# Down biases summed in the routing stage, and a last stage with three VectorE passes per tile

## What is computed

```python
h2 = rmsnorm(x, norm2_g) * (1.0 + sc2) + sh2
logits = h2 @ w_router + b_router
top_vals, top_idx = top_k(logits, 4)
weights = softmax(top_vals)
# for each token n and each of its four experts e, with weight w:
#   y[n] += w * (act(h2[n] @ w_gate_up[e] + b_gate_up[e]) @ w_down[e] + b_down[e])
x = x + gt2 * y
out = rmsnorm(x, final_norm_g)
```

## Time and profile before

| | us |
|---|---|
| median of 3 runs | 2881.35 |
| lowest and highest | 2880.42 and 2886.74 |
| profiled execution, whole time | 2879.79 |
| its span in the profile | 2877.9 |
| last stage (`phase_combine`), of the span | 2825.9 to 2877.9 |
| routing stage (`phase_route`), of the span | 1009.4 to 1037.6 |

### The profile page before, as it was taken

How to read it: one execution, slowest core, us unless ns; L and a number is a source line. 1 busy time by engine, 2 the same in 40 slices (tenths; PEclk the granted TensorE clock), 3 DMA queues, 4 the chain that set the end, 5 groups by cost and what they waited for, 6 DMA issues and landing times. The chain is left out here.

```text
span 2877.9 us, 42547 instructions
## 1 busy us (share of the span) xinstructions
PE 2649.8 (92%) x12459; PEld 2139.7 (74%) x12460; DVE 1822.0 (63%) x2667; ACT 1468.4 (51%) x2138; POOL 353.7 (12%) x428
## 2 busy tenths in 40 slices
PE   4999799996799759999999999999999999999994
PEld 4888677775677648888888888888777777887771
DVE  5332144544555576566666665666699999999995
ACT  5221144442333245555555544555587777777771
POOL 0000011101001220111111111111111111111110
PEclk7999899997799769999999999999999999999995
DMA  6652222212334276666666666666699999999975
GB/s 238 240 200 82 98 81 70 70 41 91 106 123 163 96 260 239 216 214 215 213 217 213 217 224 216 225 225 219 221 361 366 360 370 363 364 363 365 367 270 189
DMA packets 188364, 631.14 MB, mean 219 GB/s; under 512 B 24931, under 2 KB 50709, under 8 KB 170245
## 3 DMA queue, kind: packets, MB, share of 16 engines
q1 hardware_dynamic: 162240, 554.07, 52.4%
q0 software_dynamic: 24832, 71.95, 9.8%
q10 hardware_dynamic: 1220, 4.21, 0.4%
HBM read 575.44 MB, written 64.73 MB: 222 GB/s over the span
## 5 line engine op out<-in xcount | busy, mean ns | idle before, releaser
L2535 DVE TENSOR_TENSOR e_gu_lo<-gu_raw,e_gu_hi 128x1024 fp32r<-128x1024 f32 x564 | 673.5, 1219 | 176.0 <-ACT e_gu_hi L2374 148.9
L83 PE MATMUL e_pgu<-e_gu_hi,e_x_hi 128*128 128x512 f32 x1568 | 638.9, 407 | 5.6 <-DVE e_x_lo L2565 5.6
L85 PE MATMUL e_pgu<-e_gu_hi,e_x_lo 128*128 128x512 f32 x1568 | 615.6, 393 | 0.0
L84 PE MATMUL e_pgu<-e_gu_lo,e_x_hi 128*128 128x512 f32 x1568 | 613.6, 391 | 0.0
L2374 ACT ACTIVATE e_gu_hi<-gu_raw 128x1024 fp32r<-128x1024 f32 x564 | 571.7, 1055 | 29.3 <-PEq L2766 19.9
L2541 DVE TENSOR_TENSOR e_dn_lo<-dn_raw,e_dn_hi 128x1024 fp32r<-128x1024 f32 x280 | 333.0, 1218 | 16.7 <-ACT e_dn_hi L2380 16.7
L85 PEld LDWEIGHTS e_pgu<-e_gu_hi,e_x_lo 128*128 128x128 f32 x1568 | 294.9, 188 | 64.3
L83 PEld LDWEIGHTS e_pgu<-e_gu_hi,e_x_hi 128*128 128x128 f32 x1568 | 296.0, 189 | 53.2 <-issue 5.9
L84 PEld LDWEIGHTS e_pgu<-e_gu_lo,e_x_hi 128*128 128x128 f32 x1568 | 296.4, 189 | 48.2
L83 PE MATMUL e_pdn<-e_dn_hi,e_a_hi 128*128 128x512 f32 x784 | 309.1, 394 | 22.3 <-DVE e_a_lo L2569 21.6
L85 PE MATMUL e_pdn<-e_dn_hi,e_a_lo 128*128 128x512 f32 x784 | 306.4, 391 | 0.0
(11 more groups left out here) (424 smaller groups left out, 3913.9 us busy)
## 6 DMA issues: line engine op xcount, KB each, us to landing
gu_raw<-in_w_gate_up_dram SPq DMA_DIRECT2D x560, 512.0 KB, 5.6
dn_raw<-in_w_down_dram SPq DMA_DIRECT2D x140, 1024.0 KB
wada_later<-in_w_ada_dram SPq DMA_DIRECT2D x32, 512.0 KB, 4.0
gu_bias<-hidden_bias SPq DMA_DIRECT2D x42, 256.0 KB, 10.8
win_raw<-in_w_in_dram POOLq DMA_DIRECT2D x5, 2048.0 KB
proj_by_token<-out_stage SPq DMA_DIRECT2D x32, 256.0 KB, 3.1
wg_raw<-in_w_in_dram POOLq DMA_DIRECT2D x16, 512.0 KB, 4.8
gates_transposed<-g_stage POOLq DMA_DIRECT2D x32, 256.0 KB, 2.3
```

The lines of the kernel that those rows point to most:

```text
L83: pe.matmul(out, a[0], w[0], start=first, stop=False)
L84: pe.matmul(out, a[0], w[1], start=False, stop=False)
L85: return pe.matmul(out, a[1], w[0], start=False, stop=last)
L2535: dve.tensor_tensor(gu_lo[:, b, 2 * j:2 * j + 2], gu_raw[:, b, 2 * j:2 * j + 2].rearrange("p k g n -> p k (g n)"), gu_hi[:, b, 2 * j:2 * j ...
```

## The change

In `phase_out` the eight stores of zeros to the tokens' rows are gone; the one to the spare rows stays. In `phase_route` SyncE first loads `b_down` (128 KB); TensorE makes, for each of the 8 tiles, the product of turned weights and `b_down` into one PSUM tile `pb` of 1024 columns; ScalarE copies it to one of two buffers; and SyncE stores it to the tile's rows of `m.y_sum`. So the experts' scatters add to the bias sums. TensorE's first product stands before the counts' matmuls of line 1930, and the other seven behind the last weights' turn. Each product but the first waits until ScalarE has copied the one before. ScalarE's first copy stands before that of line 1922. SyncE waits for the last stores at the end of the stage.

At the end of `phase_experts` the residual of seven tiles is loaded ahead, into both halves of `gu_raw`, and `b_down` is not. In `phase_combine` TensorE has nothing to do, VectorE's add from PSUM is gone, every tile has its own `y` buffer, and all eight loads of `y` and the one of the eighth residual are issued at once.

```diff
 # phase_out, SyncE
-                sp.dma_start(m.y_sum[rows, :].rearrange("p (a n) -> p a n", a=4), zeros).then_inc(zero_out, 16)
-                if t == 0:
                     sp.dma_start(m.y_sum[SEQ:SEQ + P, :].rearrange("p (a n) -> p a n", a=4), zeros).then_inc(zero_out, 16)
...
-            sp.wait_ge(zero_out, 16 * (NT + 1))
+            sp.wait_ge(zero_out, 16)
 # phase_route
+        pb = m.psum(ctx, "pb5", [P, D])
...
         def _(sp):
+            sp.dma_start(down_bias[:], m.b_down[0]).then_inc(down_in, 16)
...
+            for t in range(NT):
+                sp.wait_ge(sum_out, t + 1)
+                sp.dma_start(m.y_sum[t * P:(t + 1) * P, :], biased[:, t % 2]).then_inc(sum_stored[t % 2], 16)
             sp.wait_ge(bias_kept, 32)
+            for b in range(2):
+                sp.wait_ge(sum_stored[b], 16 * (NT // 2))
...
         def _(act):
...
+            def keep_sums(t):
+                act.wait_ge(summed, t + 1)
+                if t >= 2:
+                    act.wait_ge(sum_stored[t % 2], 16 * (t // 2))
+                act.activation(biased[:, t % 2], pb[:], ACT.Copy).then_inc(sum_out, 1)
+            keep_sums(0)
             act.wait_ge(bias_up, 1)
             act.activation(m.bias_hl[:], braw[:], ACT.Copy).then_inc(bias_hi, 1)
+            for t in range(1, NT):
+                keep_sums(t)
...
         def _(pe):
+            def sum_biases(t):
+                if t:
+                    pe.wait_ge(sum_out, t)
+                else:
+                    pe.wait_ge(down_in, 16)
+                for half in range(2):
+                    cols = slice(half * N, (half + 1) * N)
+                    ins = pe.matmul(pb[:, cols], m.wcT[:, t], down_bias[:, cols], start=True, stop=True)
+                ins.then_inc(summed, 1)
...
             pe.matmul(pc[0:NE, 0:1], m.so_far[:, LAST], m.ones[:, 0:1], start=True, stop=True).then_inc(filled, 1)
+            sum_biases(0)
             pe.wait_ge(cum_in, 1)
...
             turn_weights(pe, m, r, LAST, 0)
+            for t in range(1, NT):
+                if t == LAST:
+                    pe.wait_ge(r.wc_kept, 1)
+                sum_biases(t)
 # phase_experts, SyncE's end
-            sp.dma_start(m.c_bd, m.b_down[0]).then_inc(once_in, 16)
             sp.dma_start(m.c_gf, m.final_g.rearrange("(a d) -> a d", a=1).to_broadcast([P, D])).then_inc(once_in, 16)
-            for t in range(2):
+            for t in range(C_AHEAD):
                 sp.dma_start(m.c_x2[:, t], m.x2[t * P:(t + 1) * P, :]).then_inc(once_in, 16)
-            wait_apart(sp, once_in, 64)
+            wait_apart(sp, once_in, 16 * C_AHEAD + 16)
 # phase_combine, with C_AHEAD = 7
         def _(sp):
             for t in range(NT):
-                b = t % 2
-                if t >= 2:
-                    sp.wait_ge(x3, t - 1)
-                sp.dma_start(y[:, b], m.y_sum[t * P:(t + 1) * P, :]).then_inc(y_in[b], 16)
-                if t >= 2:
-                    sp.dma_start(x2[:, b], m.x2[t * P:(t + 1) * P, :]).then_inc(y_in[b], 16)
...
-                    ins = pe.matmul(ps[:, t % 2, cols], m.wcT[:, t], bd[:, cols], start=True, stop=True)
-                ins.then_inc(biased, 1)
+                sp.dma_start(y[:, t], m.y_sum[t * P:(t + 1) * P, :]).then_inc(y_in[t], 16)
+            for t in range(C_AHEAD, NT):
+                sp.dma_start(late[:, t - C_AHEAD], m.x2[t * P:(t + 1) * P, :]).then_inc(x2_in, 16)
...
-                dve.tensor_tensor(acc[:, b], y[:, b], ps[:, b], ALU.add).then_inc(summed, 1)
-                dve.wait_ge(summed, t + 1)
-                dve.tensor_tensor(acc[:, b], acc[:, b], m.gate2[:], ALU.mult).then_inc(gated, 1)
+                dve.tensor_tensor(acc[:, b], y[:, t], m.gate2[:], ALU.mult).then_inc(gated, 1)
                 dve.wait_ge(gated, t + 1)
-                dve.tensor_tensor(acc[:, b], acc[:, b], x2[:, b], ALU.add).then_inc(x3, 1)
+                if t >= C_AHEAD:
+                    dve.wait_ge(x2_in, 16 * (t - C_AHEAD + 1))
+                dve.tensor_tensor(acc[:, b], acc[:, b], residual(t), ALU.add).then_inc(x3, 1)
```

More of the change, by code:

```diff
@@ L1864, in phase_route @@
         braw = sb(ctx, "r_braw", [P, FF], F32)
+        biased = sb(ctx, "r_biased", [P, 2, D], F32)
+        down_bias = sb(ctx, "r_down_bias", [NE, D], F32)
         pq = sb(ctx, "r_pq", [P, 1], F32)
@@ L1881, in phase_route @@
         bias_hi = sem("r_bias_hi")
+        down_in = sem("r_down_in")
+        summed = sem("r_summed")
+        sum_out = sem("r_sum_out")
+        sum_stored = [sem(f"r_sum_stored{i}") for i in range(2)]
         block = ctx.enter_context(nc.Block())
@@ L2640, in _ @@
             low_a(total - 1)
+C_AHEAD = 7
 def phase_combine(nc, m):
@@ L2648, in phase_combine @@
     with ExitStack() as ctx:
-        y = sb(ctx, "c_y", [P, 2, D], F32)
-        bd, gf, x2 = m.c_bd, m.c_gf, m.c_x2
+        y = sb(ctx, "c_y", [P, NT, D], F32)
+        late = sb(ctx, "c_x2", [P, NT - C_AHEAD, D], F32)
         acc = sb(ctx, "c_acc", [P, 2, D], F32)
@@ L2654, in phase_combine @@
         nrm = sb(ctx, "c_nrm", [P, NT, 4], F32)
[L2655 to L2658, removed]
+        y_in = [sem(f"c_y_in{i}") for i in range(NT)]
+        x2_in = sem("c_x2_in")
         gated = sem("c_gated")
@@ L2666, in phase_combine, with residual @@
         block = ctx.enter_context(nc.Block())
+        def residual(t):
+            return m.c_x2[:, t] if t < C_AHEAD else late[:, t - C_AHEAD]
         @block.sync
@@ L2670, in _ @@
             for t in range(NT):
-                b = t % 2
-                if t >= 2:
-                    sp.wait_ge(x3, t - 1)
-                sp.dma_start(y[:, b], m.y_sum[t * P:(t + 1) * P, :]).then_inc(y_in[b], 16)
-                if t >= 2:
-                    sp.dma_start(x2[:, b], m.x2[t * P:(t + 1) * P, :]).then_inc(y_in[b], 16)
-        @block.tensor
-        def _(pe):
-            for t in range(NT):
-                if t >= 2:
-                    pe.wait_ge(summed, t - 1)
-                for half in range(2):
-                    cols = slice(half * N, (half + 1) * N)
-                    ins = pe.matmul(ps[:, t % 2, cols], m.wcT[:, t], bd[:, cols], start=True, stop=True)
-                ins.then_inc(biased, 1)
+                sp.dma_start(y[:, t], m.y_sum[t * P:(t + 1) * P, :]).then_inc(y_in[t], 16)
+            for t in range(C_AHEAD, NT):
+                sp.dma_start(late[:, t - C_AHEAD], m.x2[t * P:(t + 1) * P, :]).then_inc(x2_in, 16)
         @block.vector
@@ L2696, in scale @@
                     dve.wait_ge(out_done[b], 16 * (t // 2))
-                dve.scalar_tensor_tensor(out=res[:, b], in0=acc[:, b], scalar=nrm[:, t, 2:3], in1=gf, op0=ALU.mult, op1=ALU.mult).then_inc(done, 1)
+                dve.scalar_tensor_tensor(out=res[:, b], in0=acc[:, b], scalar=nrm[:, t, 2:3], in1=m.c_gf, op0=ALU.mult, op1=ALU.mult).then_inc(done, 1)
             for t in range(NT):
                 b = t % 2
-                dve.wait_ge(y_in[b], 32 * (t // 2) + 16)
-                dve.wait_ge(biased, t + 1)
+                dve.wait_ge(y_in[t], 16)
                 if t >= 2:
                     dve.wait_ge(done, t - 1)
-                dve.tensor_tensor(acc[:, b], y[:, b], ps[:, b], ALU.add).then_inc(summed, 1)
-                dve.wait_ge(summed, t + 1)
-                dve.tensor_tensor(acc[:, b], acc[:, b], m.gate2[:], ALU.mult).then_inc(gated, 1)
+                dve.tensor_tensor(acc[:, b], y[:, t], m.gate2[:], ALU.mult).then_inc(gated, 1)
                 dve.wait_ge(gated, t + 1)
-                dve.tensor_tensor(acc[:, b], acc[:, b], x2[:, b], ALU.add).then_inc(x3, 1)
+                if t >= C_AHEAD:
+                    dve.wait_ge(x2_in, 16 * (t - C_AHEAD + 1))
+                dve.tensor_tensor(acc[:, b], acc[:, b], residual(t), ALU.add).then_inc(x3, 1)
                 if t:
```

4 lines of the change are left out of this document (2 added, 2 removed).

## The result

| | before | after |
|---|---|---|
| median of 4 runs each (us) | 2883.51 | 2901.77 |
| lowest, highest (us) | 2880.42, 2886.74 | 2898.07, 2903.95 |
| profiled execution (us), its span | 2879.79, 2877.9 | 2902.47, 2900.9 |

The ratio of the times is 1.0060, with a 95% interval of 1.0044 to 1.0075: slower by 12.7 to 21.6 us on 2883.5. The forecast was +16.0.

What follows compares the result with a forecast made beforehand. VectorE was taken to pace the last stage, GpSimd to end the routing stage. Terms 0, +26.2, +1.2 and -11.4 give +16.0, turning the profiled 2879.79 into 2895.8 us; 2897 was forecast for the median, range 2888 to 2904.

Steps and rivals of the forecast that it cites:

- phase_out at 0: In phase_out: dropping eight stores of zeros changes nothing, 0 us, with 0.5 us of gain as the other end.
- The routing stage, +26.2: Routing stage: seven product-and-copy rounds of 5.00 us in series, then the last store, delay the experts by 26.2 us.
- The hop from TensorE to ScalarE: Routing stage: time from TensorE's end to ScalarE's start in each round, taken as 0.15 us, between 0.05 and 0.26.
- The tail, +1.2: End of the experts' stage: longer loads share the DMA engines evenly with the last scatter, costing 1.2 us.
- third rival: Routing stage or tail: stores wait behind 6 MB of weights, or the scatter is starved for 4 us; 2900 to 2903, chance 0.12.
- The last stage, -11.4: Last stage: scalings come 4.02 us apart instead of 5.27, and the stage gains 11.4 us.
- T: Last stage: start of the first gate pass, put at 2829.05 against 2829.84, with tile 0's data there at 2829.0.
- The experts' stage, 0: Experts' stage from 1038 to 2826 us: keeps its instructions, so no change apart from its tail.
- The first (a clock that rises): Routing stage: TensorE's clock rises to 2.4 GHz, seven rounds take 22 us; +3 net, 2884.4, chance 0.08.
- The second: Routing stage: the sums are hidden under GpSimd's drain, needing rounds of 1.25 us; -10.2 us, 2871, chance 0.04.
- The fourth: Last stage: passes become bound by ScalarE; each 0.1 us beyond its cover costs 0.7 us in all; no chance given.
- cover of 0.55: Last stage: ScalarE needs 1.93 us to the next root while VectorE has passes of 2.48, leaving 0.55 us.

Runs made afterwards that it cites:

- e1: The kernel before, unedited, profiled a second time: 2879.14 us.
- e7: The changed kernel with two residual tiles loaded ahead instead of seven: 2903.99 us (one run).
- e3: The changed kernel with two PSUM buffers for the products instead of one: 2888.79 us, ratio to before 1.0031.
- e6: The changed kernel, unedited, profiled and timed again: 2898.09 us, ratio to before 1.0064.
- e10: The changed kernel with the products over 96 rows of other data instead of 32, sums wrong: 2904.30 us (one run).
- e4: The changed kernel with the products over 128 rows of other data instead of 32, sums wrong: 2889.39 us (one run).
- e8: e5 with eight buffers instead of two for the sums to be stored: 2883.15 us, ratio to before 1.0002.
- e11: The kernel before with GpSimd adding the residual, six residuals loaded ahead, products still in the last stage: 2884.03 us, ratio 1.0006.
- e2: The kernel before with only the last stage and its loads ahead changed, down biases left out: 2874.22 us, ratio 0.9973.
- e5: The changed kernel with three fp32r products packed into one for seven tiles, two made early, two PSUM buffers: 2890.32 us, ratio to before 1.0035.
- e9: The changed kernel with the products over 64 rows of other data instead of 32, sums wrong: 2903.96 us (one run).

## Why the prediction came out right

**What bounds the kernel, and phase_out at 0.** Right as far as it can be seen: up to the routing stage the two profiles differ by 1.0 us, and the thirteen by 7.6 (1007.68 to 1015.28). They fall into two groups, eight up to 1009.62 and five from 1013.47, with both kinds of kernel, zeros and none, in each; what makes the groups is open. An effect of a few us could not be seen here.

**The routing stage, +26.2, measured +25.0.** The mechanism is the one forecast: eight products, one hidden behind the counts, seven in series with their copies, clock 0.50, no copy behind a store. Two sizes were off. The hop from TensorE to ScalarE is 0.04 us (1024.23 + 3.78 = 1028.01 to 1028.05, and 1029.12 + 3.77 = 1032.89 to 1032.93), and not 0.15, so seven rounds take 34.2 us (1024.23 to 1058.46) and not 35.0: 0.8. And the first of the seven starts 15.8 us into the stage (1024.23 - 1008.41) where 16.3 had been taken (1025.72 - 1009.44): 0.5. Together they are the 1.2 or so. (Against e1's routing stage the cost is 23.7.) From the last copy's start to the experts' first work are 4.71 us, as in the sum (1.02 + 2.9 + 0.8 = 4.72).

**The tail, +1.2, measured +1.5.** e7 shows that it is the residual loads. The size came near, but not by the mechanism of the forecast. An even share of the DMA engines would have had the scatter move at half its rate beside the loads; in after nothing of it moved for the first 3.6 us behind its issue, where in before 0.20 MB had (e7). The third rival's starved scatter is nearer to what happened, though it lost 1.5 us and not 4. The near hit of this term is luck.

**The last stage, -11.4, measured -10.4.** The scalings are 3.98 apart, not 4.02, which is 0.2 in favour. The step that was off is T: the forecast took the pass to start as soon as the data had moved, 3.1 us behind the load's issue, and it started 4.4 behind it, at 2863.67. The rate of the DMA engines at the last stage's start, 40 slices of 0.25 us from 2859:

```profile
GB/s 0 0 0 0 0 16 49 147 360 311 410 426 393 459 377 426 393 377 426 410 410 426 410 443 410 410 426 426 393 442 410 426 410 410 442 426 393 410 410 426
```

Summed up, 512 KB have moved by about 2862.2, and the pass follows 1.5 us later, where the forecast had 0.05. In the kernel before that time could not be read in full, because the first pass waited for TensorE there: by the same count its data had moved by 2829.0, and it started at 2829.84. So there the load was ready within 0.84 us, and 1.5 is not a fixed price; why after needed more is open. The Trainium skill (DMA: Bandwidth & Descriptors, Anatomy of one DMA) has, for transfers that GpSimd issues, a fixed cost of about 2 us, most of it the confirmation of the last byte. This load was issued by SyncE; its 1.5 us are of that size, the 0.84 of before are under it. The store of the earlier trace rows, 2.9 us for 512 KB that move in 1.3, had shown that a transfer takes more than its move, though not at which end. About 1.2 us of the gain of 10.4 are the waits for residuals that before's profile had and e1's did not.

**The sum.** The mechanisms of the routing stage and the last stage held. That three terms which were off by up to 1.2 us came to +16.1 against +16.0 is luck: the routing stage and the last stage of the unchanged kernel differ by 1.2 or 1.3 us between before and e1.

**The experts' stage, 0, measured +7.9 in the pair.** e3 and e6 have the stored sums too and differ from before's profile by -0.2 and +1.7 there, so the 7.9 are mostly the spread of executions. A remainder of 2 to 3 us is likely by the times of more runs (e6), the forecast had no term for it, and what it would come from stays open.

**The median.** 2897.0 was given and 2901.8 came. Of the 4.8, 2.2 are the base (before's median is 2883.5 by its four runs, and was 2881.35 by the three shown), the rest is within the interval of the ratio. It is also the time that the third rival gave, and shows that a time alone doesn't pick a mechanism: in the trace of after no copy waits for a store (the cover was thin: in e10, with the same waits, the copy of tile 2 stood about 0.2 us for the store of tile 0), and the tail lost 1.5 us and not 4.

**The rivals.** The first (a clock that rises) did not occur with 32 rows; e4 shows that its mechanism is there with 128. The second would have needed rounds of 1.25 us; e8, with the products nearly off the path, still comes to 36.05, because the transfers have to pass. The fourth did not occur: in the even rounds the root was ready (2872.12 + 0.29 = 2872.41) 0.56 us before VectorE took it at 2872.97, as the forecast's cover of 0.55 has it. VectorE waited for the root only at the first scaling, 0.43 us, and at the last, 1.93, the same as in before.

**What is left over.** No kernel here beats before with the whole result; e8 and e11 are level with it. e2 puts the most that can be had by this last stage at 7.8 us, if the sums cost nothing. They would have to be stored in a stage with free time for 4 MB, such as phase_out, where leaving out the 4 MB of zeros gained nothing that these profiles show. That was not tried.

## What to carry to other kernels

Work that is moved off a bound engine is only gained if the stage that takes it has room on every resource it uses: here one tile's product was cheap and seven of them in series behind one PSUM buffer cost 25 us, and with that changed (e3, e5, e8) the next limits were the store buffers and then the bytes. Price each moved step as a chain from the event that releases it to the barrier that waits for it, the landing of its last store included. And before a difference in an untouched stage is explained, profile the same kernel twice.

## What the runs showed of the hardware

- TensorE's clock stayed at 1.2 GHz through 24.3 us of back-to-back work with 32 rows in use (e3), and through 15 us at 77% busy with 64 and 96 rows (e9, e10); with 128 rows, at the same pitch, it rose to 2.4 GHz between 1030 and 1035 us, in a chain that began at 1025.31 (e4). One run each of 64, 96 and 128 rows shows this.
- VectorE's scaling took 3.39 us in place of 1.28 beside a GpSimd addition of 2.34 on tiles of the same size; VectorE's addition with one input in PSUM kept its 1.22 us there (e11).
- A scatter that GpSimd issued while SyncE's queue had loads under way at the full rate moved none of its packets for 3.6 us (after), where it had moved 0.20 MB in that time without them (before).
- From the last data's move to the start of the pass that waits for it passed 1.5 us at the last stage's start in after, and at most 0.84 in before.
- ScalarE's waits for scatters to land were between 1.1 and 8.5 us over the experts' stage in two executions of the same program, and 15 us lay between the quickest and the slowest of 17 executions of the kernel before.
